# A two-layer attention encoder on one core: the scores of the next tile ahead of a step's first transposed piece, score passes at a step's close, new keys split two steps ahead

## The reference, cut to what matters

```python
def hybrid_layer(x, g, w_in, w_out, lq1, lk1, lq2, lk2, subln_g, rpb, lam_init):
    h = rms_norm(x, g)
    z = jnp.einsum('bsd,de->bse', h, w_in)
    qd, kd, vd, qn, kn, vn, gate = jnp.split(z, cuts, axis=-1)
    ...
    o_da = diff_attention(qd, kd, vd, lam, lam_init, subln_g)   # softmax(s0) - lam * softmax(s1), times v, RMSNorm per head
    o_na = neighbourhood_attention(qn, kn, vn, rpb)             # softmax(s + bias) over the window, times v
    o = jnp.concatenate([o_da, o_na], axis=-1) * jax.nn.silu(gate)
    return x + jnp.einsum('bse,ed->bsd', o, w_out)
```

## Time and profile before

| | |
|---|---|
| median of 3 runs | 1486.92 us (1486.36 to 1487.51) |
| the profiled execution's own time | 1487.66 us |
| its span | 1485.9 us |
| PE busy | 1434.3 us, 97% |
| DVE busy | 877.3 us, 59% |
| ACT busy | 684.4 us, 46% |
| POOL busy | 492.0 us, 33% |
| mean granted TensorE clock | 0.992 of full speed |

### The profile page before, as it was taken

The page is one execution under the profiler, slowest core; times in us unless marked ns, Lnnn a source line. Parts: engine busy times, 40 slices in busy tenths (PEclk is TensorE's granted clock), DMA queues, the critical chain, the costliest instruction groups (busy, mean ns, idle before and its releaser), DMA issues.

```text
span 1485.9 us, 23642 instructions
## 1 busy us (share of the span) xinstructions
PE 1434.3 (97%) x8160; PEld 1168.9 (79%) x8160; DVE 877.3 (59%) x1814; ACT 684.4 (46%) x1306; POOL 492.0 (33%) x384
## 2 busy tenths in 40 slices
PE   7999999999999999999999999999999999999994
PEld 6788787878788888777887878788788888887874
DVE  6666676666656565743436666766665565656423
ACT  5445454445444444652524444545454544456330
POOL 2323223133333333443643132322233333336261
PEclk9999999999999999999999999999999999999997
DMA  4700101112021111301110111000202020203112
GB/s 177 148 29 22 49 21 35 35 36 61 29 61 43 53 43 54 128 29 56 58 43 29 37 36 35 21 28 21 75 22 75 22 74 21 75 29 128 43 44 113
DMA packets 39258, 79.57 MB, mean 54 GB/s; under 512 B 18832, under 2 KB 18832, under 8 KB 39184
## 3 DMA queue, kind: packets, MB, share of 16 engines
q1 hardware_dynamic: 39184, 78.60, 16.6%
HBM read 66.57 MB, written 15.96 MB: 56 GB/s over the span
## 4 chain that ended last, share of the span: by engine, by line
PE 89%; DVE 3%; ACT 2%; issue 2%; SPq 2%; DMA 1%; POOL 0%; DVEq 0%; POOLq 0%; ACTq 0%
PE proj L956 19%; PE proj L958 17%; PE proj L957 17%; PE scores L992 10%; PE turn L1049 5%; PE mix L1101 3%; PE mix L1102 3%; PE mix L1066 2%; PE mix L1065 2%; PE mix L1067 2%; PE scores L1049 2%; SPq L485 2%; PE mix L1075 1%; ACT prob L815 1%; DVE pt_lo L1394 1%
## 5 line engine op out<-in xcount | busy, mean ns | idle before, releaser
L956 PE MATMUL proj<-h_hi,w_hi 128*128 128x512 f32 x1184 | 500.9, 423 | 11.5 <-DVE h_lo L1295 10.3
L958 PE MATMUL proj<-h_hi,w_lo 128*128 128x512 f32 x1184 | 466.3, 394 | 0.0
L957 PE MATMUL proj<-h_lo,w_hi 128*128 128x512 f32 x1184 | 463.4, 391 | 0.0
L956 PEld LDWEIGHTS proj<-h_hi,w_hi 128*128 128x128 f32 x1184 | 223.1, 188 | 75.4 <-issue 35.5
L958 PEld LDWEIGHTS proj<-h_hi,w_lo 128*128 128x128 f32 x1184 | 222.5, 188 | 51.6
L586 POOL TENSOR_TENSOR w_lo<-w_raw,w_hi 128x1024 fp32r<-128x1024 f32 x78 | 191.8, 2459 | 199.3 <-ACT w_hi L748 199.3
L957 PEld LDWEIGHTS proj<-h_lo,w_hi 128*128 128x128 f32 x1184 | 224.0, 189 | 33.9
L1386 DVE CUSTOM_DVE_ANT_0 prob<-scores,inner 128x1024 f32<-128x1024 f32 (+1 forms) x192 | 204.0, 1062 | 70.7 <-PE scores L992 69.9
L1394 DVE TENSOR_TENSOR pt_lo<-turn,pt_hi 128x512 fp32r<-128x512 f32 x208 | 139.2, 669 | 155.0 <-ACT pt_hi L790 153.5
L790 ACT ACTIVATE pt_hi<-turn 128x512 fp32r<-128x512 f32 x208 | 120.5, 579 | 222.4 <-PE turn L1049 221.7
L815 ACT ACTIVATE prob<-prob,nm,escale_now 128x1024 f32<-128x1024 f32 x128 | 158.1, 1235 | 3.3 <-DVE nm L1390 3.2
(11 more groups left out here) (162 smaller groups left out, 2268.2 us busy)
## 6 DMA issues: line engine op xcount, KB each, us to landing
w_raw<-chunks SPq DMA_DIRECT2D x81, 512.0 KB, 3.5
mixed_dram<-gate SPq DMA_DIRECT2D x28, 256.0 KB, 2.0
edge<-bias_dram SPq DMA_DIRECT2D x32, 224.0 KB, 3.9
h_lo<-mixed_dram SPq DMA_DIRECT2D x14, 512.0 KB, 6.9
xt<-x_t SPq DMA_DIRECT2D x8, 512.0 KB, 9.5
bias_dram<-bias_rows SPq DMA_DIRECT2D x16, 240.0 KB, 6.1
out_t<-prob SPq DMA_DIRECT2D x6, 512.0 KB, 3.0
out_t<-gate SPq DMA_DIRECT2D x2, 512.0 KB, 3.0
```

What stands on the lines that cost most here:

```text
L956: pe.matmul(dst, a_hi, b_hi, start=start, stop=False)
L957: pe.matmul(dst, a_hi, b_lo, start=False, stop=False)
L958: return pe.matmul(dst, a_lo, b_hi, start=False, stop=stop)
```

## The change

Five things move; none is added or removed.
- TensorE: the scores of the tile after (`following`: tile t+1, in step 7 tile 0 of the next group, in step 8 none) are issued in step t behind `fill(0)` and directly ahead of the first transposed piece. Before, the scores of tile t stood at the head of step t. So the scores are issued six projection matmuls short of a whole step earlier. `sum_pair` stands behind `fill(0)`, `spread_factor` moves from the end of an odd step into the next even one, ahead of the scores.
- VectorE: the two score passes of tile t+1 close step t, behind both `pt_lo`; before, those of tile t opened step t. `combine` moves between the first and the second `pt_lo`.
- ScalarE: the exponential of map c comes ahead of `pt_hi` of piece c; before it came behind.
- The new keys are split in step 6 instead of step 7 (on VectorE behind both `pt_lo` and ahead of the score passes).
- Of the last group's gate, pieces (1, 2, 1 chunks) instead of (1, 1, 2) go to the three fills of step 8.

```diff
-    GATE_HEAD = [range(0, 1), range(1, 2), range(2, 4)]
+    GATE_HEAD = [range(0, 1), range(1, 3), range(3, 4)]
...
+        def following(g, behind, t):
+            if t < NT - 1:
+                return g, t + 1
+            return (behind, 0) if t == NT - 1 and behind else None
...
# ScalarE, attend
-                    if g.project and t == NT - 1:
-                        k_hi_part(g)
...
-                    if not g.na and t % 2 and t >= 3:
-                        mean_square(g, (t - 3) // 2)
...
                     for c in range(2):
+                        if front:
+                            exponentials(front, ft, c)
+                        if c == 0 and not g.na and t % 2 and t >= 3:
+                            mean_square(g, (t - 3) // 2)
+                        if c == 1 and g.project and t == NT - 2:
+                            k_hi_part(g)
                         p_part(g, t - 1, c)
...
-                        if front:
-                            exponentials(front, ft, c)
# TensorE, step
-                if front and ft != 1:
-                    score(front, ft)
...
                 fill(0)
+                if not g.na and t % 2 and t >= 3:
+                    sum_pair(g, (t - 3) // 2)
+                if not g.na and t % 2 == 0 and t >= 4:
+                    spread_factor(g, t // 2 - 2)
+                if following(g, behind, t):
+                    score(*following(g, behind, t))
                 turn_p(g, t - 1, 0)
# VectorE, step
-                if front:
-                    for m in range(2):
-                        shifted(front, ft, m)
...
+                    if c == 0 and front:
+                        combine(front, ft)
...
-                    if g.project and t == NT - 1 and c == 0:
-                        k_lo_part(g.group() + 1)
-                if front:
-                    combine(front, ft)
+                if g.project and t == NT - 2:
+                    k_lo_part(g.group() + 1)
+                if following(g, behind, t):
+                    shift_scores(*following(g, behind, t))
...
+                if t == NT and behind:
+                    shift_scores(behind, 1)
```

More of the change, by code:

```diff
@@ L1144, in step @@
                     parts = [range(4, 5), range(5, 8), ()]
-                if not g.na and t % 2 and t >= 3:
-                    sum_pair(g, (t - 3) // 2)
                 if t == NT and behind and not behind.project:
@@ L1171, in step @@
                     weigh(g, t - 1)
-                elif not g.na and t >= 3:
-                    spread_factor(g, (t - 3) // 2)
                 if last_step:
@@ L1466, in step, with shift_scores @@
             def step(g, behind, t, front, ft, ended=None):
-                if front:
+                def shift_scores(g, t):
                     for m in range(2):
-                        shifted(front, ft, m)
+                        shifted(g, t, m)
                 def add_pieces(slot):
@@ L1537, in _ @@
                 piece_part(g, 0)
+                for c in range(2):
+                    shifted(g, 1, c)
                 from_second(dve, l, step)
```

## The result

The changed kernel takes 1631.73 us (median of 4 runs, 1628.52 to 1634.24) against 1486.64 (4 runs, 1485.75 to 1487.51): ratio 1.0975, 95% interval 1.0949 to 1.1. That is 145 us more; 130 were forecast. The time lies 2 us above the range of 1603 to 1630 that the prediction gave three chances in four, and inside its wider range of 1592 to 1634. The profiled execution has a span of 1632.2 us, 146.3 more than before, at a mean granted clock of 0.967 instead of 0.992.

A forecast was written before the change was run, and what follows sets the result against it. PE, busy 97% of the span, was taken to bound the kernel. Waits of +79 us in DA and +38 in NA, -4 for switches and +17 for the clock gave +130, forecast 1616 us, range 1603 to 1630.

The forecast's parts named there:

- The steady odd step: From odd into even DA steps, PE waits 0.64 us for VectorE's read of the scores before, 16 times, 10 us.
- Step 2: DA group start: scores wait 4.0 us (3.0 in two groups), 30 us; second piece 0.9 and weigh 0.35, 10 us.
- Step 7: DA group end: sum_pair waits 1.1 us, the next group's scores behind q_lo 0.6 more; 14 us in all.
- Step 8: DA group end: second transposed piece waits 3.4 us, weigh some 0.7 more; 28 us in all.
- The small waits of DA: Waits of weigh in steady even steps (3 us), and of the second piece or weigh in steps 2 and 8.
- NA: NA groups' starts and ends and the last groups: waits sum to 50 us, less 12 already there, +38.
- The clock: Half of the waits of 2 us and more bring a dip to 1.2 GHz: 11 x 1.5 = 17 us.
- The transposed piece behind scores: Scores now left for a transposed piece, not a projection, in 112 steps: taken as 0, bounds -11 and +11 us.
- one term without a row: 8 us estimated as already waited in the last groups before the change, taken off NA's new waits.
- The clock stays at full speed: Rival: the waits come but the clock does not fall, 1600 us; chance 0.15.
- Falls after nearly every gap: Rival: clock falls at nearly every gap and the last group's tail costs its upper bound, 1645 us; chance 0.07.
- Faster: Rival: earlier scores give softmax slack, old waits go, 1467 us; chance 0.02 (b: start of a step's second transposed piece).

The follow-up runs named there:

- e4_busy: Changed kernel plus 13 unread matmuls ahead of the second transposed piece of step 8 in six DA groups: 1632.9 us, ratio 1.0987.
- e7_group_start: Kernel before; step 1: exponentials before pt_hi, combine between both pt_lo; step 2: first pt_lo between score passes, w_hi behind first pt_hi: 1466.69 us.
- e6_orders_back_late: Changed kernel with exponentials, combine and projected pieces at their old places, scores behind the second transposed piece: 1511.97 us, ratio 1.0185.

## Why the prediction was right, and where its terms were off

**What bounds the kernel, and the direction.** Right. PE had no slack, and the new waits were paid in full: 108.9 us of new idle time. PE's busy share of 90% and the mean clock of 0.967 are those forecast too (near 90%, about 0.97).

**The steady odd step.** Forecast 0.64 us, 16 times; measured 0.61, and 0.69 from start to start. Right.

**Step 2.** Forecast 4.0 us for the scores; the stretch from the second piece's end on, 257.03 to 262.42, is 5.39 us where the six matmuls take 1.45, so the wait is 3.94 (the trace puts 3.75 on the releaser). Right.

**Step 7.** Forecast 1.1 for `sum_pair`, measured 8.4 us for 8 in the list, 1.05 each and at most 1.2. The scores behind `q_lo`: forecast 0.6 in DA and 0.5 in NA, 8.8 in all; measured 9.3.

**Step 8.** Forecast 3.4, measured 3.48. Right.

**The small waits of DA: too large on paper.** `weigh` in the steady even steps (0.2 us, 16 times) stands in the list once, with 0.17. In step 2 the second piece (0.9) does not wait and `weigh` waits 0.6 instead of 0.35; in step 8 it waits 0.4 and not 0.7. Together some 12 us that did not come. In step 2 the reason is in the rows: PE runs through that stretch at 1.2 GHz (263.60 to 267.00 above) and comes later to the piece than I had it come. Of the eight step-2 waits one is not followed by a fall, and in that group both the piece and `weigh` wait (0.9 and 0.35 forecast):

```profile
870.78 0.66 PE L1056 MATMUL turn<-ident,prob 128*128 128x128 f32 x4 [0.65 <-DVE pt_lo L1401]
...
874.84 0.38 PE L1072 MATMUL mix<-pt_hi,v_hl 128*128 128x256 f32 x1 [1.31 <-DVE pt_lo L1401]
```

**NA.** The scores at a group's start, forecast 2.3:

```profile
515.67 0.50 PE L999 MATMUL scores<-k_hi,q_hi 64*128 64x512 f32 x2 [2.32 <-DVE mx L1393]
```

In the first NA group of a layer it is 1.4 only. The third piece, forecast 1 to 2.4 and 9 us in all, has 8.8 us in six waits of at most 2.4.

**The clock: mechanism right, the term wrong twice, and the two errors nearly cancel by luck.** The prediction had 11 falls at 1.5 us each. The trace shows 26 lengths of 3.4 us, more than double. Their price can be estimated from groups that do the same work with more or fewer falls: between the values' transpositions of one DA group and the next it is 94.25 us with 3.4 us at the lower clock, 95.45 and 95.28 with 6.8, and 96.89 with 13.65. That is 0.26 us per us at the lower clock, 0.88 for each 3.4; the groups that lead to NA give 0.9 (92.62 with 6.8, 94.43 with 13.65), and the same groups in e4_busy 0.74 (92.34 with 3.4, 94.57 with 13.65). These are pairs that lie far apart. Others scatter: in e4_busy two DA groups with 10.24 us take 95.83 and 95.64, and two with 6.83 take 95.80 and 95.65, no difference. So the price is an estimate from few groups, and it depends on where the falls lie. I had taken 1.5, since only a small part should fall on waiting. But in this kernel the ends of the waits are set by VectorE: matmuls that run slower arrive at a wait that is shorter by as much. So 26 lengths at 0.74 to 0.9 are 19 to 23 us, an estimate, against 17 forecast.

The Trainium skill ("TensorE: Matmul & The Clock Gate", section "HAM oscillation — how this bites in real kernels") has the clock fall again at each gap between bursts. The rows bear this out better than my half did. The prediction had counted 22 to 24 waits of 2 us and more; there are 22, 14 in DA and 8 in NA. With 19 of them a fall begins within the wait or at most 1.5 us behind its end; with three (ending at 142.6, 333.8 and 865.8) none does. The other three falls follow shorter waits: the one at 222.7 comes behind two of 1.15 and 0.47 us. In e4_busy it was a later gap that was followed by the longer fall. The same section of the Trainium skill counts the whole of the speed lost as time; in this kernel it was about half.

**The transposed piece behind scores.** It was put at 0 with bounds of 11 us on either side. Measured:

```profile
277.80 0.66 PE L1056 MATMUL turn<-ident,prob 128*128 128x128 f32 x4
278.21 0.48 PE L963 MATMUL proj<-h_hi,w_hi 128*128 128x512 f32 x1
...
280.37 0.60 PE L1056 MATMUL turn<-ident,prob 128*128 128x128 f32 x4
280.73 0.48 PE L963 MATMUL proj<-h_hi,w_hi 128*128 128x512 f32 x1
```

The piece behind the scores takes 0.41 us until the next kind starts, the other 0.36: 0.05 in each of 112 steps, +6 us. The joined run of 15 projection matmuls takes 3.54 us (280.73 to 284.27); before, 9 took 2.17 and the 6 behind the scores 1.50, so 0.13 is saved in a pair of steps, more than the 0.06 forecast. Where the scores then wait, as in the steady DA steps, PE only comes earlier to its wait.

**The sum: one term without a row, and one that hides another.** Of the 146.3 us, 108.9 are idle time and 37.4 busy time.

The idle time first, with the list of waits taken group by group. DA's waits come to 79 us where 95 were forecast; 16.3 of before go, so DA adds 62 and not 79. NA's and those at the layers' ends come to 51 us where 50 were forecast. From these 50 the prediction took 12 for waits that are there already: 4.0 of the list, and 8 that it estimated for the last groups. The list of before has no such 8 us. NA thus adds 47 and not 38, and this estimate is the term of the sum that was most wrong. (The bounds of 22 and 48 do not follow either: 4 and 16 in each layer give 26 and 50.)

The busy time: the 22 falls hold 83.6 us of PE's busy time, where the one of before holds 3.4. In a fall a 512-column matmul comes every 0.43 us (240.27 to 240.70), otherwise every 0.23 (239.33 to 239.56). So 0.47 of these 80 us are lost speed, an estimate of 37 us, which is all of the growth. The changes between kinds of matmul then come to about nothing instead of the -4 forecast, since the piece behind the scores costs 6 and the joined fills win 8. A steady pair of DA steps shows the same: 20.60 us (276.21 to 296.81) against 19.97 before, 0.63 more, where the new wait alone is 0.69; 20.8 were forecast.

Since the falls cost only 19 to 23 us net, 14 to 18 of the 37 came back out of waits, as in step 2; that is about what DA's waits fall short. Without falls the idle time would have grown by 123 to 127 us, where 79 + 38 = 117 were forecast. Of the 16 us between the span's growth and the forecast's 130, 6 to 10 are thus waits, which are the 8 without a row, 4 the changes between matmuls, and 2 to 6 the clock. These shares are estimates; the modelled ends of matmuls do not allow closer ones.

**The rivals.** "The clock stays at full speed" (1600) is refuted by 22 falls. "Falls after nearly every gap" (1645) has its mechanism nearly right, 19 of 22, and its price too high. "Faster" (1467) needed the scores free at b + 4.24 in odd steps and b + 1.83 in step 2; the two waits above are those distances. That 1467 is where e7_group_start ended is no support for it: that kernel gets rid of the same 16.3 us of waits without moving any scores.

**What stays open.** Which gaps are followed by a fall and which not: filling one gap moved the others. What the move of `w_hi` in e7_group_start is worth by itself. And which changes between matmuls cost e6_orders_back_late its 9.3 us of busy time.

## What to carry to other kernels

Where one engine is busy 97% of the span, an instruction moved earlier in its queue is worth nothing unless the engine that frees its buffer does so earlier too; write both orders side by side from a common start and take the later of the two, at the steady step and at each irregular one, since four irregular places per group cost more here than all steady steps. Look first at the waits that the list names, and at all the orders that feed one of them: four small moves against 16.3 us of waits won 17 to 18 us, and one or two of them alone less than half of it. Before taking off waits that "are there already", find them in the list: 8 us taken off without a row were half of this forecast's error. In a kernel whose waits other engines end, charge a fall of TensorE's clock at about half of the speed it takes away (here 0.74 to 0.9 of 1.7 us), and count one for nearly every new gap of the sizes seen here.

## What the hardware showed that was not expected

- Falls of the clock do not belong to single gaps. With the wait of step 8 filled (PE busy 6.55 of 7.00 us at clock 1.00), the fall behind it went, and that of step 2 doubled; time at the lower clock went from 111.1 to 104.2 us and the kernel's time did not change (1631.73 and 1632.9 us).
- 3.4 us at 1.2 GHz cost an estimated 0.74 to 0.9 us of the kernel's time, where the speed lost is 1.7 us; some groups of e4_busy show no difference for 3.4 us.
- A transposed piece directly behind 64-row score matmuls takes 0.05 us more than one behind 128-row projection matmuls (0.41 against 0.36).
